# Recurrence of a hybrid block: a new order of TensorE's small and large groups of products

## Chip, cores, metric

One Trainium2 chip (trn2), one core. The metric is the device time of one execution in microseconds.

## The reference, cut to what matters

One layer for 1024 tokens of width 1024: RMSNorm, one input projection, an RWKV-7 group (8 heads of 64) beside a sliding-window attention group, an output projection, a SwiGLU feed-forward, a final norm. The change lies in the RWKV-7 recurrence:

```python
def step(S, inp):
    r_t, w_t, k_t, v_t, kk_t, a_t = inp
    sa = jnp.einsum('bhvk,bhk->bhv', S, -kk_t)
    S = (S * w_t[:, :, None, :]
         + sa[..., None] * (kk_t * a_t)[:, :, None, :]
         + v_t[..., None] * k_t[:, :, None, :])
    return S, jnp.einsum('bhvk,bhk->bhv', S, r_t)
...
o = (o - mean) * lax.rsqrt(var + GN_EPS)
```

## The kernel before, in words

The scan is done in 8 token tiles (t = 0 to 7) of 128 tokens. Within a tile the recurrence is a triangular system: NB and KB hold, for each head, the masked products of keys with queries (part 0) and with the removal keys (part 1); the inverse of the triangular part is built from 16x16 blocks on VectorE (`lanes`, the block inverse), and grown on TensorE to 32 (corners 1, updates 1: y1 and x1) and 64 (corners 2, updates 2: y2). U solves the tile, S is the state, O the output.

All engines run their own instruction list, written out by hand; semaphores order them. PSUM has eight banks, and a plan (`C`) gives each job of a tile a bank: O always has bank 5, R bank 0, t1 bank 1, U and t2 bank 2, y1 and y2 bank 4, x1 bank 6. `C.claim` lets TensorE wait until the reader of the job before in that bank has emptied it; `C.result` lets a reader wait for the products; `C.emptied` waits for the reader.

TensorE in tile t (`stage5_tensor`): products of the state with alpha into R (L1497); a filler, `busy`, a matmul with the identity that nobody reads (L1456); corners 1 (L1416), which wait for X; KB's products with V, part 1, into R (L1491); the claim of O; updates 1 (y1, then x1, L1416); the running sums of the decay gates for tile t+2 (`cumulative`, L1250, which reads sgt); part 0 of KB's products for heads 0 to 3 into O; corners 2; part 0 for heads 4 to 7; updates 2 (y2); the state with rho into O; `outputs(t-1)`, four transposes (L1468); U in two halves with the corrections of R between (L1542 to L1565); the new state (L1576); O's last products (L1582); the masks' raw products for later tiles (L1262).

VectorE in tile t (`stage5_vector`): Ts1 from corners 1 (L1658); `moments(t-1)`, which reads and empties O's bank (a sum, L1743, and the centred oc, L1746); `first_updates` of X and XT (L1664, L1665); `variance(t-1)` (L1754), which waits for ScalarE's squares of oc; `prepare(t+2)` (L1288 to L1294), which waits for ScalarE's exponentials of the running sums; `lanes(t+1)`; `gated`; the state's sum (L1776); the masks of KB for t+1 and of NB for t+2 (L1312).

ScalarE copies between: squares, R's low half, the exponentials, Ts2 from corners 2, XT from y2 (`last_updates`, L1606 and L1607), U and R.

SP's queue issues the transfers through DRAM: `gather` takes NB's diagonal blocks to the lanes (LA), `scatter` takes the inverse blocks (LM) to X and XT, and between them sgt (gates of tile t+2) and vtk (V of tile t+1) are loaded. GpSimd makes the reciprocal root of the variance, `on` and `mix`.

Of the kernel before, what the change touches and what calls it, by code (L numbers as in the profile page):

```python
# [17 lines left out]
NT = T // P  # L18
KD = D // P
HD = 64  # L20
H = 8
# [55 lines left out]
def hybrid_block(nc, x_t, par_in, w_in, w0, w_up, a_up, g_up, sinks, w_out, w_gate_up, w_down, norm_final_g,  # L77
# [13 lines left out]
    sg_dram = nc.dram_tensor("sg_scratch", (T, W), F32, kind="Internal").ap()  # L91
# [7 lines left out]
    with root:  # L99
# [1132 lines left out]
        def tok(t):  # L1232
            return slice(t * P, (t + 1) * P)
# [82 lines left out]
        def stage5_sync(sp):  # L1316
            def gather(t):

                for g in range(4):
                    C.emptied(sp, f"b{g}", t)  # L1320
                if t:
                    sp.wait_ge(s_lane, 16 * t)
                for q in range(2):
                    r = slice(q * HD, (q + 1) * HD)
                    sp.dma_start(bass.AP(d_n.tensor, q * (P + 1) * HD, [[P, HD], [8 * IMG, H], [1, HD]]),
                                 NB[t % 2][r, :, 1, r]).then_inc(s_img, 16)
                sp.wait_ge(s_img, 32 * t + 32)
                if t:
                    sp.wait_ge(s_inv16, t)
                sp.dma_start(LA[:, 0:BLK * BLK].rearrange("p (i j) -> p i j", i=BLK),  # L1330
                             bass.AP(d_n.tensor, 0, [[IMG, 64], [P, BLK], [1, BLK]])).then_inc(s_lane, 16)

            def scatter(t):
                sp.wait_ge(s_inv16, t + 1)
                if t:
                    sp.wait_ge(s_xt, 32 * t)
                sp.dma_start(bass.AP(d_i.tensor, 0, [[IMG2, 64], [P, 2 * BLK], [1, BLK]]),
                             LM.rearrange("p (r j) -> p r j", j=BLK)).then_inc(s_img2, 16)
                if t:
                    C.result(sp, "t2", t - 1)  # L1340
                else:
                    A.result(sp, "rn", NT - 1)
                sp.wait_ge(s_img2, 16 * t + 16)
                for m, o, done in ((X, P, s_xl), (XT, 0, s_xt)):
                    if t and m is XT:
                        C.result(sp, "U", t - 1)
                    for q in range(2):
                        sp.dma_start(m[q * HD:(q + 1) * HD, :, :],
                                     bass.AP(d_i.tensor, o + q * (2 * P + 1) * HD, [[2 * P, HD], [8 * IMG2, H], [1, HD]])
                                     ).then_inc(done, 16)  # L1350

            A.result(sp, f"sc{NP - 1}", NT - 1)
            sp.dma_start(sgt[:, :], sg_dram[tok(1), :]).then_inc(s_sgt, 16)
            sp.wait_ge(s_vd, 16 * NT)
            sp.dma_start(vtk_[0][:, :], v_dram[tok(0), :]).then_inc(s_vtk, 16)
            gather(0)
            scatter(0)
            for t in range(NT):
                if t + 2 < NT:
                    C.result(sp, "cum1", t + 1)  # L1360
                    sp.dma_start(sgt[:, :], sg_dram[tok(t + 2), :]).then_inc(s_sgt, 16)
                if t + 1 < NT:
                    gather(t + 1)
                    sp.wait_ge(s_vtk, 16 * t + 16)
                    if t:
                        C.result(sp, "S", t - 1)
                    sp.dma_start(vtk_[(t + 1) % 2][:, :], v_dram[tok(t + 1), :]).then_inc(s_vtk, 16)
                    scatter(t + 1)

        def cleared(pool, first, end):  # L1370
# [31 lines left out]
        def stage5_tensor(pe):  # L1402
# [6 lines left out]
            def blocks_of(b, count, lhs, rhs, groups):  # L1409

                n = len(groups) * H
                for h in range(H):
                    for g in groups:
                        lo, ro = lhs(g, h), rhs(g, h)
                        to = g[2]
                        mm = pe.matmul(b[32 * to:32 * to + 32, h * count:(h + 1) * count] if len(ro.shape) == 2 else  # L1416
                                       b[32 * to:32 * to + 32, h * count:(h + 1) * count].rearrange("p (a w) -> p a w", a=2),
                                       lo, ro, start=h == 0, stop=h == H - 1, skip_group_check=True)
                return mm

            def rows(g):
                return slice(32 * g, 32 * g + 32)
# [15 lines left out]
            def updates(n, t):  # L1438
                C.emptied(pe, f"t{n}", t)
                if n == 1:  # L1440
                    b = C.claim(pe, "y1", t)
                    C.done(blocks_of(b, 32, lambda g, h: Ts1[rows(g[0]), h, :],
                                     lambda g, h: XT[rows(g[0]), h, :].rearrange("p (a w) -> p a w", a=2)[:, :, 16:32], FOUR),
                           "y1", t)
                    b = C.claim(pe, "x1", t)
                    C.done(blocks_of(b, 16, lambda g, h: XT[rows(g[0]), h, 0:32],
                                     lambda g, h: Ts1[rows(g[0]), h, 0:16], [(0, 0, 0), (2, 0, 2)]), "x1", t)
                else:
                    C.emptied(pe, "y1", t)
                    b = C.claim(pe, "y2", t)  # L1450
                    C.done(blocks_of(b, 32, lambda g, h: Ts2[rows(g[0]), h, :],
                                     lambda g, h: XT[rows(g[0]), h, 32:64], [(1, 0, 0), (3, 0, 2)]), "y2", t)

            def busy(b, n):
                for _ in range(n):
                    pe.matmul(b[:, :], ident, cst[:, 0:HALF], start=True, stop=True)  # L1456
# [26 lines left out]
            for t in range(NT):  # L1483
# [5 lines left out]
                def products_of(b, part, *hs):  # L1489
                    for h in hs:  # L1490
                        mm = pe.matmul(b[:, h * HD:(h + 1) * HD], KB[:, h, part, :], vtk[:, h * HD:(h + 1) * HD],  # L1491
                                       start=part == 0 and h == 0, stop=False, skip_group_check=True)
                    return mm
# [12 lines left out]
                if not more:  # L1506
                    C.emptied(pe, "S", t - 1)
                    busy(bank[3], 3)
                if t:
                    if more:  # L1510
                        busy(C.claim(pe, "t1", t), 1)
                    corners(1, t)
                pe.wait_ge(s_vtk, 16 * t + 16)
                for g in range(4):
                    C.emptied(pe, f"k{g}", t)
                products_of(br, 1, *range(H)).then_inc(s_r, 1)
                bo = C.claim(pe, "O", t)
                if t == 0:
                    corners(1, t)
                    products_of(bo, 0, *range(4))  # L1520
                    busy(C.claim(pe, "S", t), 1)
                pe.wait_ge(s_xt, 32 * t + 32)
                updates(1, t)
                if t + 2 < NT:
                    cumulative(pe, t + 2)
                if t:
                    products_of(bo, 0, *range(4))
                corners(2, t)
                products_of(bo, 0, *range(4, H))
                updates(2, t)  # L1530
                if more:
                    of_state(bo, rho, False)
                else:
                    busy(bank[3], 1)
                if t:
                    outputs(t - 1)

# [115 lines left out]
        def stage5_vector(dve):  # L1653
# [75 lines left out]
                       "ot", t)  # L1729

            lanes(0)
            dve.wait_ge(s_z5, 6)
            masked(dve, "k", KB, 0, 0, 1)
            prepare(dve, 1)
            masked(dve, "k", KB, 0, 2, 3)
            A.emptied(dve, "pv", NT - 1)
            A.emptied(dve, "g", NT - 1)
            dve.wait_ge(s_gm, NT)
# [18 lines left out]
            for t in range(NT):  # L1757
                first_corners(t)
                if t:
                    moments(t - 1)  # L1760
                first_updates(t)
                if t:
                    variance(t - 1)
                if t + 2 < NT:
                    prepare(dve, t + 2)
                if t + 1 < NT:
                    lanes(t + 1)
                if t:
                    gated(t - 1)
                if t + 1 < NT:  # L1770
                    b = C.result(dve, "S", t)
                    if t:
                        dve.wait_ge(s_S, t)
                    for e in range(2):
                        r = slice(HD * e, HD * e + HD)
                        ins = dve.tensor_tensor(Sn[r, :, r], b[r, :].rearrange("p (a n) -> p a n", a=NP)[:, :, r],  # L1776
                                                S[r, :, r], ALU.add)
                    C.read(ins, "S", t)
                    masked(dve, "k", KB, t + 1, 0, 1, 2, 3)
                if t + 2 < NT:  # L1780
                    masked(dve, "b", NB[t % 2], t + 2, 0, 1, 2, 3)
# [918 lines left out]
```

## Time and profile before

| what | value |
|---|---|
| median of the three runs | 1307.79 us (1307.63 to 1317.0) |
| profiled execution | 1302.4 us, its span 1300.6 us |
| TensorE matmul busy | 1258.5 us, 97% of the span |
| VectorE, ScalarE, GpSimd busy | 830.2, 480.0, 271.8 us |
| granted TensorE clock, mean | 0.988 |
| recurrence (tiles 0 to 7) | about 354 to 552 us from the span's start |

The profile is one execution. "Idle before, <-releaser" in a timeline is how long the engine stood still before the row and who let it go on; "issue" means that nothing in the profile shows what it waited for. A float32 matmul is shown as two records. Rows of the timeline merge neighbouring records (xN).

### The profile page before, as it was taken

How to read it: one execution, taken by the hardware profiler on the slowest of the kernel's cores; microseconds unless marked ns; L12 is line 12 of the kernel's file. 1: busy time of each engine (PE TensorE's matmuls, PEld its weight loads, DVE VectorE, ACT ScalarE, POOL GpSimd, SP SyncE). 2: the span in 40 equal slices, each digit the busy share in tenths (PEclk: the TensorE clock that was granted, in tenths of full speed). 3: DMA queues.
4: the chain of work that ended last, by engine and by line, in shares of the span. 5: the costliest groups of instructions: out<-in, count | busy, mean ns of one | idle time of the engine just before them, and what ended most of it. 6: DMA issues, size and time to landing. Idle time of an engine off the chain costs nothing.

```text
span 1300.6 us, 20575 instructions
## 1 busy us (share of the span) xinstructions
PE 1258.5 (97%) x8219; PEld 1027.6 (79%) x8219; DVE 830.2 (64%) x1247; ACT 480.0 (37%) x863; POOL 271.8 (21%) x210
## 2 busy tenths in 40 slices
PE   7999999988899999999999999999999999999996
PEld 6888888655588888788878888888888888888885
DVE  6866622289868867554575666567677776547765
ACT  6100032398433323333453333333333334334335
POOL 0576600034302112100005233233223300000001
PEclk9999999999999989999999999999999999999998
DMA  5576632300232232332212321333554577766643
GB/s 218 188 249 216 224 107 100 116 1 8 50 65 49 62 69 54 126 155 98 86 54 87 98 77 70 98 100 111 194 174 142 170 274 273 235 212 211 213 142 138
DMA packets 117627, 172.80 MB, mean 133 GB/s; under 512 B 55328, under 2 KB 59424, under 8 KB 117280
## 3 DMA queue, kind: packets, MB, share of 16 engines
q1 hardware_dynamic: 117536, 171.54, 40.0%
q8 instruction: 63, 1.03, 0.3%
q14 instruction: 28, 0.23, 0.1%
HBM read 119.57 MB, written 51.39 MB: 131 GB/s over the span
## 4 chain that ended last, share of the span: by engine, by line
PE 83%; DVE 8%; DMA 4%; ACT 3%; issue 1%; SPq 0%; DVEq 0%; ACTq 0%
PE bank L2368 28%; PE bank L363 21%; PE bank L2472 14%; PE bank L1491 2%; PE bank L377 2%; PE bank L468 2%; PE bank L1416 2%; PE bank L1262 2%; DMA hid_scratch<-rt 1%; PE bank L1497 1%; PE bank L986 1%; DVE scores L1172 1%; PE bank L1456 1%; DMA inv_scratch<-LM 1%; DMA X<-inv_scratch 1%
## 5 line engine op out<-in xcount | busy, mean ns | idle before, releaser
L2368 PE MATMUL bank<-thi,ahi 128*128 128x512 f32 x320 | 124.5, 389 | 0.0
L2368 PE MATMUL bank<-tlo,ahi 128*128 128x512 f32 x320 | 124.5, 389 | 0.0
L2368 PE MATMUL bank<-thi,alo 128*128 128x512 f32 x320 | 124.5, 389 | 0.0
L2472 PE MATMUL bank<-ch,dwh 128*128 128x512 f32 x308 | 120.3, 391 | 0.4 <-DVE dwl L2046 0.4
L2472 PE MATMUL bank<-ch,dwl 128*128 128x512 f32 x308 | 119.9, 389 | 0.0
L2472 PE MATMUL bank<-cl,dwh 128*128 128x512 f32 x308 | 119.8, 389 | 0.0
L342 DVE TENSOR_TENSOR ring_wlo<-ring_raw,ring_whi 128x1024 fp32r<-128x1024 f32 x30 | 40.5, 1350 | 122.1 <-ACT ring_whi L336 122.1
L363 PE MATMUL bank<-hhi,ring_whi 128*128 128x512 f32 x288 | 114.4, 397 | 0.0
L363 PE MATMUL bank<-hhi,ring_wlo 128*128 128x512 f32 x288 | 112.2, 390 | 0.0
L363 PE MATMUL bank<-hlo,ring_whi 128*128 128x512 f32 x288 | 112.1, 389 | 0.0
L2368 PE MATMUL bank<-x1hi,ahi 128*128 128x512 f32 x240 | 93.4, 389 | 0.0
L2368 PE MATMUL bank<-x1lo,ahi 128*128 128x512 f32 x240 | 93.4, 389 | 0.0
L2368 PE MATMUL bank<-x1hi,alo 128*128 128x512 f32 x240 | 93.4, 389 | 0.0
L336 ACT ACTIVATE ring_whi<-ring_raw 128x1024 fp32r<-128x1024 f32 x30 | 31.6, 1056 | 152.5 <-PE bank L363 142.2
L2042 ACT ACTIVATE dwh<-dwr 128x1408 fp32r<-128x1408 f32 x28 | 38.7, 1381 | 114.1 <-PE bank L2472 107.8
L2368 PEld LDWEIGHTS bank<-tlo,ahi 128*128 128x128 f32 x320 | 60.1, 188 | 12.6
L2368 PEld LDWEIGHTS bank<-thi,ahi 128*128 128x128 f32 x320 | 60.1, 188 | 12.5
L2368 PEld LDWEIGHTS bank<-thi,alo 128*128 128x128 f32 x320 | 60.1, 188 | 12.4
L2472 PEld LDWEIGHTS bank<-ch,dwh 128*128 128x128 f32 x308 | 57.8, 188 | 12.8 <-DVE dwl L2046 0.8
L2472 PEld LDWEIGHTS bank<-ch,dwl 128*128 128x128 f32 x308 | 57.8, 188 | 12.2
L2472 PEld LDWEIGHTS bank<-cl,dwh 128*128 128x128 f32 x308 | 57.8, 188 | 11.7
L363 PEld LDWEIGHTS bank<-hhi,ring_whi 128*128 128x128 f32 x288 | 54.1, 188 | 11.9 <-issue 1.0
(341 smaller groups left out, 2805.4 us busy)
## 6 DMA issues: line engine op xcount, KB each, us to landing
hraw<-hid_scratch SPq DMA_DIRECT2D x12, 1024.0 KB, 6.3
hid_scratch<-hid SPq DMA_DIRECT2D x22, 512.0 KB, 6.3
hid_scratch<-rt SPq DMA_DIRECT2D x11, 1024.0 KB, 4.7
dwr<-down_sums SPq DMA_DIRECT2D x16, 704.0 KB, 4.1
ring_raw<-in_w_in SPq DMA_DIRECT2D x20, 512.0 KB, 4.1
raw_a<-in_w_gate_up SPq DMA_DIRECT2D x20, 512.0 KB, 4.0
raw_b<-in_w_gate_up SPq DMA_DIRECT2D x20, 512.0 KB, 5.2
dwr<-in_w_down SPq DMA_DIRECT2D x12, 704.0 KB, 4.2
```

The lines of the kernel that those rows point to most:

```text
L336: act.activation(self.ring.hi[:, s, 0:self.kt, :], self.ring.raw[:, s, 0:self.kt, :], ACT.Copy).then_inc(self.ring.hi_ready, 1)
L342: dve.tensor_tensor(self.ring.lo[:, s, 0:self.kt, :], self.ring.raw[:, s, 0:self.kt, :], self.ring.hi[:, s, 0:self.kt, :].bitcast(F32), AL ...
L363: mm = pe.matmul(o[:, :], wpart[:, s, k, :], apart[:, k, c], start=i == 0, stop=i == n - 1)
L377: mm = pe.matmul(bank[self.J.bank_of[f"{s}{half}"]][:, :], wpart[:, s, ks[n], :], apart[:, ks[n], c], start=n == 0 and i == 0, stop=n == l ...
L468: mm = pe.matmul(b[:, :], wpart[:, s, k, :], apart[:, k, c], start=k == 0 and i == 0, stop=k == KD - 1 and i == 2)
L986: mm = pe.matmul(bank[6][HD * e:HD * e + HD, p * P:(p + 1) * P], vt[:, t + j, (p // 2) * HD:(p // 2 + 1) * HD], pt[:, p % 2, j, e, :], sta ...
L1262: mm = pe.matmul(b[e][:, i * 2 * P:(i + 1) * 2 * P].rearrange("p (a n) -> p a n", a=2), src[r, 2 * g + i, tok(t)], rho_alpha(t, r, 2 * g + ...
L1416: mm = pe.matmul(b[32 * to:32 * to + 32, h * count:(h + 1) * count] if len(ro.shape) == 2 else b[32 * to:32 * to + 32, h * count:(h + 1) * ...
L1491: mm = pe.matmul(b[:, h * HD:(h + 1) * HD], KB[:, h, part, :], vtk[:, h * HD:(h + 1) * HD], start=part == 0 and h == 0, stop=False, skip_g ...
L2042: act.activation(dw_hi[m % 2][:, :, :], dw_raw[m % 2][:, :, :], ACT.Copy).then_inc(ring2.hi_ready, 1)
L2368: mm = pe.matmul(b[:, :], w[:, k, :], m[:, k, :], start=opens and k == 0 and i == 0, stop=not (j, n) in parts and k == 3 and i == 2, skip_ ...
L2472: mm = pe.matmul(b[:, :], w[m % 2][:, k, :], a[:, k, :], start=opens and k == 0 and i == 0, stop=name not in PART2 and k == KF - 1 and i = ...
```

## The change

TensorE: corners 1 move behind KB's part 1; the filler before them (tiles 1 to 6) goes; part 0 for heads 0 to 3 moves up behind corners 1 and the claim of O; x1's update moves behind the running sums; part 0 for heads 4 to 7 moves ahead of corners 2; updates 2 move behind the state's products with rho. VectorE: `prepare(1)` moves ahead of the first masks, `variance(t-1)` ahead of `first_updates(t)`. SP: sgt for tile t+3 is issued between vtk and the scatter of tile t+1, instead of that for t+2 ahead of the gather.

```diff
@@ -1353,18 +1353,22 @@
             sp.dma_start(sgt[:, :], sg_dram[tok(1), :]).then_inc(s_sgt, 16)
             sp.wait_ge(s_vd, 16 * NT)
             sp.dma_start(vtk_[0][:, :], v_dram[tok(0), :]).then_inc(s_vtk, 16)
+            def gates(t):
+                C.result(sp, "cum1", t - 1)
+                sp.dma_start(sgt[:, :], sg_dram[tok(t), :]).then_inc(s_sgt, 16)
+
             gather(0)
             scatter(0)
+            gates(2)
             for t in range(NT):
-                if t + 2 < NT:
-                    C.result(sp, "cum1", t + 1)
-                    sp.dma_start(sgt[:, :], sg_dram[tok(t + 2), :]).then_inc(s_sgt, 16)
                 if t + 1 < NT:
                     gather(t + 1)
                     sp.wait_ge(s_vtk, 16 * t + 16)
                     if t:
                         C.result(sp, "S", t - 1)
                     sp.dma_start(vtk_[(t + 1) % 2][:, :], v_dram[tok(t + 1), :]).then_inc(s_vtk, 16)
+                    if t + 3 < NT:
+                        gates(t + 3)
                     scatter(t + 1)
 
         def cleared(pool, first, end):
@@ -1442,14 +1446,16 @@
                     C.done(blocks_of(b, 32, lambda g, h: Ts1[rows(g[0]), h, :],
                                      lambda g, h: XT[rows(g[0]), h, :].rearrange("p (a w) -> p a w", a=2)[:, :, 16:32], FOUR),
                            "y1", t)
-                    b = C.claim(pe, "x1", t)
-                    C.done(blocks_of(b, 16, lambda g, h: XT[rows(g[0]), h, 0:32],
-                                     lambda g, h: Ts1[rows(g[0]), h, 0:16], [(0, 0, 0), (2, 0, 2)]), "x1", t)
                 else:
                     C.emptied(pe, "y1", t)
                     b = C.claim(pe, "y2", t)
                     C.done(blocks_of(b, 32, lambda g, h: Ts2[rows(g[0]), h, :],
                                      lambda g, h: XT[rows(g[0]), h, 32:64], [(1, 0, 0), (3, 0, 2)]), "y2", t)
+
+            def update_of_x(t):
+                b = C.claim(pe, "x1", t)
+                C.done(blocks_of(b, 16, lambda g, h: XT[rows(g[0]), h, 0:32],
+                                 lambda g, h: Ts1[rows(g[0]), h, 0:16], [(0, 0, 0), (2, 0, 2)]), "x1", t)
 
             def busy(b, n):
                 for _ in range(n):
@@ -1506,32 +1512,27 @@
                 if not more:
                     C.emptied(pe, "S", t - 1)
                     busy(bank[3], 3)
-                if t:
-                    if more:
-                        busy(C.claim(pe, "t1", t), 1)
-                    corners(1, t)
                 pe.wait_ge(s_vtk, 16 * t + 16)
                 for g in range(4):
                     C.emptied(pe, f"k{g}", t)
                 products_of(br, 1, *range(H)).then_inc(s_r, 1)
+                corners(1, t)
                 bo = C.claim(pe, "O", t)
+                products_of(bo, 0, *range(4))
                 if t == 0:
-                    corners(1, t)
-                    products_of(bo, 0, *range(4))
                     busy(C.claim(pe, "S", t), 1)
                 pe.wait_ge(s_xt, 32 * t + 32)
                 updates(1, t)
                 if t + 2 < NT:
                     cumulative(pe, t + 2)
-                if t:
-                    products_of(bo, 0, *range(4))
+                update_of_x(t)
+                products_of(bo, 0, *range(4, H))
                 corners(2, t)
-                products_of(bo, 0, *range(4, H))
-                updates(2, t)
                 if more:
                     of_state(bo, rho, False)
                 else:
                     busy(bank[3], 1)
+                updates(2, t)
                 if t:
                     outputs(t - 1)
 
@@ -1729,10 +1730,9 @@
                        "ot", t)
 
             lanes(0)
+            prepare(dve, 1)
             dve.wait_ge(s_z5, 6)
-            masked(dve, "k", KB, 0, 0, 1)
-            prepare(dve, 1)
-            masked(dve, "k", KB, 0, 2, 3)
+            masked(dve, "k", KB, 0, 0, 1, 2, 3)
             A.emptied(dve, "pv", NT - 1)
             A.emptied(dve, "g", NT - 1)
             dve.wait_ge(s_gm, NT)
@@ -1758,9 +1758,8 @@
                 first_corners(t)
                 if t:
                     moments(t - 1)
+                    variance(t - 1)
                 first_updates(t)
-                if t:
-                    variance(t - 1)
                 if t + 2 < NT:
                     prepare(dve, t + 2)
                 if t + 1 < NT:
```

## Rows read from the trace of the kernel before

**Rows 1.** The page: busy time, share of the span and instructions of each engine.

```profile
PE 1258.5 (97%) x8219; PEld 1027.6 (79%) x8219; DVE 830.2 (64%) x1247; ACT 480.0 (37%) x863; POOL 271.8 (21%) x210
```

**Rows 2.** Stretches, one per tile (3, 4, 5): length, busy (instructions), clock, DMA.

```profile
429.30:453.80 24.50, 23.73 (x409) 20.73 (x407) 19.41 (x42) 7.85 (x22) 4.65 (x4) 1.00 0.31 67
453.80:483.20 29.40, 28.30 (x409) 25.00 (x407) 19.50 (x42) 7.83 (x22) 4.49 (x4) 0.83 0.34 77
483.20:506.90 23.70, 23.60 (x408) 20.70 (x406) 19.40 (x42) 7.85 (x22) 4.65 (x4) 1.00 0.18 35
```

**Rows 3.** Timeline of PE, tile 3: start, length, line, operation, idle before.

```profile
430.27 1.02 PE L1456 MATMUL bank<-cst 128*128 128x512 f32 x2
431.97 0.72 PE L1416 MATMUL bank<-X,NB 32*32 32x16 f32 x64 [0.67 <-DMA X<-inv_scratch]
432.67 1.97 PE L1491 MATMUL bank<-vtk,KB 128*128 128x64 f32 x16
434.62 0.72 PE L1416 MATMUL bank<-XT,Ts 32*32 32x32 f32 x62
...
435.78 1.16 PE L1250 MATMUL bank<-cst,sgt 128*128 128x129 f32 x8
436.77 1.00 PE L1491 MATMUL bank<-vtk,KB 128*128 128x64 f32 x8
...
439.36 0.69 PE L1416 MATMUL bank<-XT,Ts 32*32 32x32 f32 x32
439.99 1.16 PE L1497 MATMUL bank<-S,arv 128*128 128x128 f32 x8
441.05 0.63 PE L1468 MATMUL bank<-cst,on 128*128 128x128 f32 x4
```

**Rows 4.** Timeline of DVE in tile 3.

```profile
432.89 0.35 DVE L1658 TENSOR_SCALAR Ts<-bank,cst 128x128 f32<-128x128 f32 x1 [1.34 <-PE bank L1416]
433.16 0.68 DVE L1743 TENSOR_REDUCE sm<-bank 128x8 f32<-128x512 f32 x1
433.88 0.69 DVE L1746 SCALAR_TENSOR_TENSOR oc<-sm,bank 128x512 f32<-128x512 f32 x1
...
438.11 0.69 DVE L1288 TENSOR_TENSOR ab<-ab,einv 128x512 f32<-128x512 f32 x1 [0.94 <-ACT einv L1279]
...
448.28 0.37 DVE L1718 COPY LM<-LV 64x256 f32<-64x256 f32 x1
```

**Rows 5.** Timeline of PE: waits for X, and gaps by issue.

```profile
382.76 0.72 PE L1416 MATMUL bank<-X,NB 32*32 32x16 f32 x64 [0.73 <-DMA X<-inv_scratch]
...
386.58 0.22 PE L1416 MATMUL bank<-XT,Ts 32*32 32x32 f32 x3 [0.48 <-issue]
...
407.52 0.72 PE L1416 MATMUL bank<-X,NB 32*32 32x16 f32 x64 [0.25 <-DMA X<-inv_scratch]
...
460.60 0.20 PE L1416 MATMUL bank<-Ts,XT 32*32 32x16 f32 x2 [0.94 <-issue]
```

**Rows 6.** Timeline of ACT in tile 3: second copy of y2.

```profile
440.49 0.37 ACT L1607 ACTIVATE XT<-bank 32x256 f32<-32x256 f32 x1
```

**Rows 7.** Timeline of SP's queue: X for tile 4.

```profile
451.97 1.27 SPq L1348 DMA_DIRECT2D X<-inv_scratch  x2
```

**Rows 8.** Timeline of all engines, at the start of the recurrence.

```profile
347.47 1.35 DVE L1312 COPY_PREDICATED KB<-cst,bank 128x512 f32<-128x512 uint32 x2 [1.21 <-PE bank L1262]
...
351.25 3.29 PE L1262 MATMUL bank<-arv,ab 64*128 64x256 f32 x16 [1.79 <-DVE arv L1292]
```

**Rows 9.** Stretches in which the granted clock was at half.

```profile
461.00:471.00 10.00, 10.00 (x101) 9.30 (x101) 8.27 (x23) 2.71 (x11) 3.22 (x3) 0.50 0.18 35
...
515.60:519.00 3.40, 3.40 (x44) 3.17 (x38) 3.12 (x12) 0.75 (x2) 1.71 (x2) 0.50 0.14 42
...
539.50:543.00 3.50, 3.50 (x36) 1.92 (x28) 0.00 (x0) 1.80 (x3) 1.63 (x2) 0.51 0.48 159
...
351.90:355.20 3.30, 3.30 (x15) 2.10 (x12) 2.47 (x5) 0.00 (x0) 0.00 (x0) 0.50 0.74 182
```

## The prediction

> **What bounds the kernel now.** I read the page first. TensorE (PE) is busy 1258.5 us of a span of 1300.6 [rows 1], so whatever moves the time must shorten or lengthen PE's own queue. Everything that is changed lies in the recurrence, between 346 and 552 us. The table of stretches, one per token tile, says how a tile is bounded [rows 2]: tile 3 lasts 24.5 us with PE busy 23.73, tile 5 lasts 23.7 with 23.60. VectorE (DVE) is busy 19.4 of them and ScalarE 7.9. Tile 4 has the same instructions (409) and lasts 29.4 us: its granted clock is 0.83. So a tile costs PE's work at the full clock, some short waits, and now and then a stretch at half clock.
>
> The timeline of PE in tile 3 shows the order [rows 3]: a filler of 1.02 us, 0.67 us of idleness until X has landed, the first corners (431.97 to 432.67), KB's products by V (1.97 us), then the y1 and x1 products, the running sums (1.16), half of O's products, the second corners, the other half, y2, the state's products, the transposes, and U. At the same time DVE does, in this order, Ts1 from the corners (432.89) and then the moments of the tile before, 433.16 to 434.57 [rows 4]. The moments are what frees the bank of O, and they stand behind Ts1 in DVE's queue. In the kernel before, PE spends exactly this time on KB's products: they end at 434.6.
>
> **The change, part by part.** All sums are against the profiled execution, 1302.4 us.
>
> *Fillers out.* One filler in each of tiles 1 to 6 goes: start to start 1.0 us [rows 3], so -6.0 us of PE's time.
>
> *Corners behind KB's products.* KB's masks are made before the tile begins, so KB's 1.95 us can run right behind the alpha products, while X still lands. X was waited for 0.73, 0.25 and 0.67 us in tiles 1, 2, 3 [rows 3, 5]; KB's products, 1.95 us in place of the 1.0 us filler, cover that: -1.65.
> But right behind the corners now stands the claim of O's bank, then half of O's products. The claim waits for the moments of tile t-1, and those wait in DVE's queue behind Ts1, which waits for these same corners. By the row of DVE the moments end at 434.57 where the corners ended at 432.67 [rows 3, 4], so PE stands still for 1.9 us and the handover (0.05: one row ends at 351.19 for a start at 351.25): 1.95 us. What is queued behind that claim is all of PE's tile: O, y1, the sums, everything. The work that hid the moments has been moved in front of the corners and nothing took its place. +1.95 in each of tiles 1 to 7 = +13.65. From both sides: it can't be under 1.0 unless the moments shrink (two passes of 0.68 and 0.69 that have to be made after Ts1), and is at most 2.1.
>
> *Y2 last but one.* y2 now comes behind the state's products; between y2 and U stand the transposes alone. ScalarE copies y2 into XT until 440.86, that is 1.5 us from the start of y2 at 439.36 [rows 3, 6]. Before, the state's products and the transposes (1.06 + 0.6) covered that. Now y2 itself (0.6) and the transposes (0.6) are 1.2 us: U waits +0.3 us in tiles 1 to 7, and 0.9 in tile 0, which has no transposes: +3.0. Bounds 1.5 and 4.
>
> *x1 behind the running sums, variance before the first updates.* The sums come 0.6 us sooner after y1, x1's update as much later; the first updates end about 5.9 us after the corners, where the exponentials that preparation waits for are ready too, against 5.4 before [rows 4]. Variance waits for ScalarE's squares, in a time in which DVE had nothing to do. Nothing of it is on PE's path: 0. The cover is the DVE's slack before X, next.
>
> *The loop through X.* Corners of t, Ts1, y1, sums, exponentials, preparation, the block inverse (ends 448.65), scatter, X at 451.97 issued and about 4 us later landed [rows 4, 7]: at present 23.9 to 24.5 us. With the 1 us wait and the shifts above it becomes about 24.8 us from corners to corners. PE's own tile becomes 23.85 - 1.0 + 1.95 + 0.3 = 25.1. So X is no longer late; the loop costs nothing, and would take over only if DVE's part grew by 0.4 us.
>
> *sgt a tile ahead.* Its issue (0.62) moves on SP's queue from before the gather to between vtk and the scatter. There it waits for the sums of tile t+2, which PE has made some 12 us before the scatter's own release; so the scatter isn't delayed. Before, the gather began right after B's masks, not after sgt. 0, bounds -0.3 and +0.3.
>
> *Preparation moved up, at the start.* DVE idles 1.21 us, makes two masks (347.47 to 348.8), then prepares tile 1; PE idles 1.79 us until that ends [rows 8]. With preparation (2.5 us) begun at 346.25 it ends at 348.8, and the two masks, which then gate PE through the banks, end at 350.15: -1.1 us. The clock was at half for 3.3 us right behind that idleness (351.9 to 355.2, [rows 9]); if the shorter idleness spares that, -1.5 more. I take -2.6, bounds 0 and -2.8.
>
> *The gaps without a releaser.* PE stood 0.48 and 0.94 us inside the run of y1 and x1 products (96 small matmuls in a row), with nothing that released it [rows 5]. With large groups between, I take both as gone: -1.4; bounds -1.4 and +1. The Trainium skill ("Runtime: NRT & Kernel Launch", instruction fetch mechanics) says that straight code is fetched ahead and that this is hidden; by that rule the gaps have another cause, and splitting the groups removes nothing: the sum would be 1.4 us more. The row, two gaps where matmuls are shortest and none in large groups, speaks rather for a supply that runs short.
>
> At full clock the sum is -6.0 - 1.65 + 13.65 + 3.0 - 2.6 - 1.4 = +5.0 us.
>
> *The clock.* This is the large and uncertain term. The granted clock went from full (2.4 GHz) to half (1.2) four times [rows 9]: after the 1.79 us of idleness; in tile 4, after KB's products, y1, x1 and the 0.94 us gap, and then for 10 us; in tiles 6 and 7 for 3.4 and 3.5 us after y1, x1, half of O, the second corners, half of O and with no idleness. What these have in common is small products, half-loaded groups of O or KB, and short idleness, close together; tiles 1 to 3, which had less of it, kept the full clock. The change puts into every tile KB's products, corners, 1.95 us of nothing, half of O and y1 in a row: 6 us with less work than what preceded each fall. So I expect a fall in most tiles, in spite of the spread small groups. Price of a fall: half of its length, 1.7 us (3.4 at half clock) to 5.0 us (10 us). The nearest row is tile 4's, since the new fall too comes ahead of the sums and the second half of O, not just before the state's products: 5.0. I take five such falls in the seven tiles, +25, in place of the three of before (5.0 + 1.7 + 1.75 = 8.45). Net +16.5; bounds -8.45 (no fall at all) and +26.5 (seven long ones).
>
> Sum: 1302.4 + 5.0 + 16.5 = 1324 us. The profiled run was 5.4 us below the median of the runs shown, 1307.79; against that median the forecast is +1.2%.
>
> **Rivals.**
> *The clock behaves as before.* The 1.95 us wait is there, but spreading the small groups offsets it: two or three falls of the old sizes. Then 1302.4 + 5.0 = 1307, no change. For it: tile 1 had 0.73 us of idleness and a 0.48 us gap around the corners and kept its clock [rows 5]. Against: the new hole is 2.7 times as long. It decides from about three long falls down.
> *No fall at all.* 1307.4 - 8.45 = 1299, -0.7%. This is what the order would give if small groups in a row were the only cause of the falls.
> *The hole isn't there.* This is the other side: PE doesn't wait for the moments, because DVE gets at them early enough or O's bank is free. Mechanism: only the claim of bank 5; price: 13.65 us less and then also no new falls: 1299 - 13.65 = 1285, and the loop through X, 24.2 us a tile, then binds and gives back some 6 us: about 1291, -1.3%. It turns on one thing, DVE's order of Ts1 and moments, and the rows speak against it.
> *Every tile falls long.* 1302.4 + 5.0 - 8.45 + 35 = 1334.
>
> **How the numbers follow.** Forecast (falls in most tiles, 1316 to 1340 with its bounds) 0.60; clock as before 0.25; no fall 0.10; no hole 0.05. The range has to reach into the second case: 1303 to 1340. A measurement of this kernel tells about 1% from no change, which is 1294.7 to 1320.9. Within the forecast's case about a tenth ends below 1320.9. Slower 0.55, within 1% 0.39, faster 0.06.
>
> **What the profile after would show.** PE idle about 1.9 us in front of O's products by V in tiles 1 to 7, released by DVE's oc; no wait for X; U waiting about 0.3 us for XT; PE's idleness at 350 us shorter by 1.1; stretches of tiles 1 to 5 of 25 us where the clock is 1.00 and 28 to 31 where it isn't; gaps by issue gone. I am wrong if the clock row shows 1.00 in most tiles, or if the claim of O's bank isn't waited for.

## The result, and the profile after

The changed kernel takes 1357.64 us (median of 4 runs, 1350.11 to 1366.22) against 1312.39 for the one before (median of 4 runs, 1307.63 to 1318.85), a ratio of 1.034 (95% interval 1.025 to 1.044). The ratios here and below are of fast executions: those more than 1.5% above the fastest of their kernel are left out. The profiled execution took 1351.6 us, 49.2 more than that of before (1302.4).

The stretches of the recurrence by tile, changed kernel, tiles 0 to 6 (length; busy us of PE, PEld, DVE, ACT, POOL with instructions; granted clock; DMA share; GB/s), answer to [rows 2]:

```profile
355.00:379.20 24.20, 23.20 (x403) 20.27 (x401) 14.01 (x35) 7.21 (x21) 0.00 (x0) 1.00 0.27 61
379.20:415.80 36.60, 34.75 (x407) 31.27 (x405) 18.68 (x42) 7.96 (x22) 4.17 (x4) 0.63 0.25 53
415.80:442.50 26.70, 24.48 (x407) 21.85 (x405) 18.62 (x42) 7.84 (x22) 4.17 (x4) 0.94 0.18 39
442.50:472.50 30.00, 28.08 (x412) 25.17 (x411) 19.32 (x43) 7.84 (x22) 4.15 (x4) 0.83 0.31 68
472.50:508.00 35.50, 33.65 (x401) 30.36 (x399) 17.79 (x41) 7.96 (x22) 4.15 (x4) 0.62 0.22 45
508.00:536.00 28.00, 25.78 (x418) 23.07 (x414) 19.90 (x45) 7.73 (x22) 4.15 (x4) 0.94 0.20 42
536.00:570.00 34.00, 31.54 (x375) 27.66 (x375) 15.02 (x34) 5.30 (x12) 4.15 (x4) 0.60 0.20 42
```

Read the clock column first, then the length: PE's work is about the same in tiles 1 to 5 (401 to 418 records), tile 0 at full clock takes 24.2 us, and no tile from 1 on stays at 1.00. VectorE is busy 17.8 to 19.9 us in each of tiles 1 to 5, whatever their length. The whole stage, changed kernel:

```profile
354.00:601.00 247.00, 231.69 (x3146) 202.68 (x3145) 134.90 (x288) 61.97 (x157) 29.99 (x28) 0.75 0.24 57
```

and before:

```profile
354.00:552.00 198.00, 192.73 (x3166) 164.96 (x3162) 139.31 (x289) 61.62 (x157) 32.30 (x28) 0.95 0.30 70
```

These two rows hold the result: 49 us more between about the same two points of the program, with PE idle 15 instead of 5 us, and the other 39 us of the growth in busy time of the same work (six fillers less) at a lower clock.

PE's timeline in tile 1, changed kernel (answers to [rows 3]; the last bracket is the idle time before the row and its releaser):

```profile
380.21 1.90 PE L1497 MATMUL bank<-vtk,KB 128*128 128x64 f32 x16
382.03 0.72 PE L1420 MATMUL bank<-X,NB 32*32 32x16 f32 x64
384.61 1.97 PE L1497 MATMUL bank<-vtk,KB 128*128 128x64 f32 x8 [1.85 <-DVE oc L1746]
386.51 1.08 PE L1420 MATMUL bank<-XT,Ts 32*32 32x32 f32 x64
387.52 2.09 PE L1250 MATMUL bank<-cst,sgt 128*128 128x129 f32 x8
389.54 1.04 PE L1420 MATMUL bank<-Ts,XT 32*32 32x16 f32 x32
390.50 1.75 PE L1497 MATMUL bank<-vtk,KB 128*128 128x64 f32 x7
```

and DVE's in the same place (answers to [rows 4]):

```profile
382.89 0.35 DVE L1659 TENSOR_SCALAR Ts<-bank,cst 128x128 f32<-128x128 f32 x1 [1.40 <-PE bank L1420]
383.16 0.68 DVE L1743 TENSOR_REDUCE sm<-bank 128x8 f32<-128x512 f32 x1
383.87 0.69 DVE L1746 SCALAR_TENSOR_TENSOR oc<-sm,bank 128x512 f32<-128x512 f32 x1
```

KB's products, the corners, then 1.85 us of nothing, until the moments have emptied O's bank at 384.56. Half of O's products takes 1.97 us for the 8 records that take 1.00 in [rows 3]: the clock has fallen inside the hole. The stretches around the fall and the rise:

```profile
383.00:384.00 1.00, 0.00 (x0) 0.00 (x0) 0.97 (x3) 0.00 (x0) 0.00 (x0) 1.00 0.69 148
384.00:385.00 1.00, 0.39 (x2) 0.39 (x3) 0.56 (x1) 0.35 (x1) 0.00 (x0) 0.73 0.48 100
385.00:411.00 26.00, 26.00 (x279) 23.32 (x278) 11.98 (x31) 5.99 (x18) 4.17 (x4) 0.50 0.24 49
411.00:412.00 1.00, 1.00 (x7) 1.00 (x7) 1.00 (x2) 1.00 (x4) 0.00 (x0) 0.61 0.00 0
```

For 26 us PE is busy without a break, and at half clock (1.2 GHz). A stretch whose clock reads 0.73 was at half clock for 0.54 of its microsecond; such parts are added up here. Taken over one-microsecond stretches from 346 to 609 us, the changed kernel is at half clock for 129.7 us: 27.3, 3.4, 10.2, 27.3, 3.4, 27.3 and 30.7 us, one fall in each of tiles 1 to 7. The kernel before has 23.9 us: five falls, four of them of 3.4 us. The prediction knew four; the fifth, at 553 us, comes behind the recurrence.

The start of the recurrence, changed kernel (answers to [rows 8]):

```profile
351.27 2.00 PE L1262 MATMUL bank<-arv,ab 64*128 64x256 f32 x16 [0.67 <-DVE KB L1312]
```

The wait for preparation is 0.67 in place of 1.79 us, and the products behind it take 2.00 in place of 3.29 us: no fall there. That the shorter wait spared the fall isn't shown. The kernel before without its fillers (below) waits the old 1.79 us and has no fall either:

```profile
351.18 2.00 PE L1262 MATMUL bank<-arv,ab 64*128 64x256 f32 x16 [1.79 <-DVE arv L1292]
```

### The profile page after: what moved, and what is told of

It reads as the page before. It is cut to its first block, busy times and chain, and to the rows that moved or that the text cites. A ratio compares the mean times of both kernels' runs of the same rounds, so it can differ in the third digit from the quotient of the medians.

```text
span 1349.8 us, 20544 instructions
## 1 busy us (share of the span) xinstructions
PE 1300.3 (96%) x8207; PEld 1068.0 (79%) x8207; DVE 826.0 (61%) x1247; ACT 480.5 (36%) x863; POOL 271.1 (20%) x210
## 3 DMA queue, kind: packets, MB, share of 16 engines
q8 instruction: 63, 1.03, 0.3%
## 4 chain that ended last, share of the span: by engine, by line
PE 92%; DVE 5%; ACT 2%; issue 1%; DMA 1%; DVEq 0%; SPq 0%; ACTq 0%
PE bank L2367 28%; PE bank L363 21%; PE bank L2471 16%; PE bank L1497 3%; PE bank L1262 3%; PE bank L1420 2%; PE bank L377 2%; PE bank L468 2%; PE bank L1503 2%; PE bank L1583 1%; PE bank L1250 1%; PE bank L986 1%; PE bank L1543 1%; PE bank L1566 1%; PE bank L1557 1%
## 5 line engine op out<-in xcount | busy, mean ns | idle before, releaser
L363 PEld LDWEIGHTS bank<-hlo,ring_whi 128*128 128x128 f32 x288 | 54.1, 188 | 12.0 <-issue 1.0
```

The source lines that it names most:

```text
L363: mm = pe.matmul(o[:, :], wpart[:, s, k, :], apart[:, k, c], start=i == 0, stop=i == n - 1)
```

## The experiments

Each ratio is to the kernel before, run beside it on the same chip. Three chips were used, on which the kernel before took 1310.4, 1305.7 and 1310.3 us, so ratios compare better than times. Half-clock times are those of one profiled execution each, between 346 and 609 us. **Theory A**: the hole in front of O's products is the cause of both the waiting and the falls. **Theory B**: the clock falls because the fillers are gone and small and half-loaded groups alternate, whatever the hole. **Theory C**: the waiting costs more than its length by its place.

**One part alone: corners behind KB's products, fillers kept** (on the kernel before).

```diff
-                if t:
-                    if more:
-                        busy(C.claim(pe, "t1", t), 1)
-                    corners(1, t)
+                if t and more:
+                    busy(C.claim(pe, "t1", t), 1)
...
+                corners(1, t)
                 bo = C.claim(pe, "O", t)
+                products_of(bo, 0, *range(4))
...
```

> The kernel before with one part of the change alone: corners 1 behind KB's products, and the first half of O's products right behind the claim, fillers kept, all else as before. Theory A: the whole loss appears, hole of 1.9 us in each of seven tiles (+12 after the waits for X that it hides) and long stretches at half clock: 1330 to 1350 us. Theory B (fillers taken out are what the clock misses): clock as before, about 1315 us.

Measured: 1360.26 us, ratio 1.040 (1.032 to 1.048). PE in tile 1:

```profile
384.63 1.89 PE L1491 MATMUL bank<-vtk,KB 128*128 128x64 f32 x16
386.46 0.73 PE L1416 MATMUL bank<-X,NB 32*32 32x16 f32 x64
388.97 1.97 PE L1491 MATMUL bank<-vtk,KB 128*128 128x64 f32 x8 [1.78 <-DVE oc L1742]
```

The same hole in all seven tiles, and the whole loss, with every filler in its place: 119.5 us at half clock, a fall in each of tiles 1 to 7 and one at the start. A's range (1330 to 1350 us) was too low by 10 us at its upper end. Missing fillers aren't the main cause: they were kept, and the clock fell as in the changed kernel.

**The other part alone: fillers out** (on the kernel before).

```diff
                 if t:
-                    if more:
-                        busy(C.claim(pe, "t1", t), 1)
                     corners(1, t)
```

> The kernel before without its fillers in tiles 1 to 6, nothing else. Theory A (what counts is idleness next to small groups): the 1.0 us of the filler turns mostly into waiting for X (the loop through X stays 24 us), so the full-clock time falls by 1 to 2 us at most and the half-clock stretches grow somewhat: 1300 to 1320 us. Theory B (the missing fillers are what the clock lacks): half-clock stretches of over 80 us as in the changed kernel, 1335 to 1355 us.

Measured: 1305.08 us, ratio 1.000 (0.996 to 1.004). What PE does where the filler was, tile 1:

```profile
378.64 1.16 PE L1497 MATMUL bank<-S,arv 128*128 128x128 f32 x8
381.17 0.71 PE L1416 MATMUL bank<-X,NB 32*32 32x16 f32 x64 [1.37 <-DMA X<-inv_scratch]
```

The filler turned into waiting for X, 0.9 to 1.4 us in five tiles. Half clock: 30.7 us against 23.9. This idleness in front of the corners cost next to nothing, as A had it (1300 to 1320 us).

**Everything but TensorE's order** (TensorE as before; preparation 1, variance and sgt as changed).

> The changed kernel with TensorE's order of before: of the change only preparation 1 ahead of the masks, variance ahead of the first updates and sgt a tile ahead are left. All theories: the loss is in TensorE's order, so this is the kernel before less 1.1 to 2.6 us at the start, 1303 to 1312 us. If sgt's or variance's move had a share in the loss, it would show here as over 1320 us.

Measured: 1306.0 us, ratio 1.000 (0.995 to 1.005). None of these three has a share in the loss. The start's gain isn't visible over the spread of the runs: this profile has one fall of 23.9 us in tiles 3 and 4, with TensorE's order of before and no hole. One of the ten runs took 4370.27 us, and one of the ten without fillers 2514.9; the cause of these two isn't known.

**The hole filled** (changed kernel, two fillers in front of the claim).

```diff
                 corners(1, t)
+                if t:
+                    busy(C.claim(pe, "S", t) if more else bank[3], 2)
                 bo = C.claim(pe, "O", t)
```

> The changed kernel with two filler matmuls (about 1.9 us at full clock) between the corners and the claim of O, in tiles 1 to 7: TensorE's queue is as long as with the hole, but it isn't idle. Theory A: the full-clock length stays (the wait turns into fillers), the half-clock stretches go: 1351.6 - 35 = 1310 to 1322 us. Theory C (the waiting itself, by its place in the chain, costs more than its length): stays above 1335 us.

Measured: 1303.21 us, ratio 0.995 (0.992 to 0.999); profiled execution 1301.3 us. From tile 4 to the end of the stage:

```profile
455.10:551.00 95.90, 93.06 (x1550) 77.02 (x1548) 64.46 (x130) 30.77 (x70) 17.52 (x16) 1.00 0.32 80
```

The clock doesn't fall between 346 and 609 us. PE's queue is as long as with the hole (tile 1 is 25.3 us from one tile's alpha products to the next's; forecast for the hole 25.1), and 50 us are gone (1351.6 to 1301.3). This separates the two prices: with the hole's time kept and PE busy in it, the loss of the falls, 50 us, is gone. C is out: as much time is spent at the same place, and the extra loss is gone. B isn't tested here, since fillers are back; the moments first, below, tests it. The measured time lies below A's range (1310 to 1322 us), which had the clock at 35 us.

**Half of the hole filled** (one filler in the same place).

> The changed kernel with one filler (about 1 us) between the corners and the claim of O in tiles 1 to 7: about 0.85 us of the 1.85 us hole is left idle, the full-clock length is the same as with the whole hole or with two fillers. Theory A with a price that follows the idle time: half-clock stretches in between, some 30 to 60 us, 1315 to 1335 us. If only a long hole makes the clock fall: as with two fillers, about 1303 us.

Measured: 1303.9 us, ratio 0.996 (0.992 to 0.999). PE in tile 1, and the stage from tile 1 on:

```profile
381.28 0.73 PE L1420 MATMUL bank<-X,NB 32*32 32x16 f32 x64
381.94 1.13 PE L1462 MATMUL bank<-cst 128*128 128x512 f32 x2
383.87 1.10 PE L1497 MATMUL bank<-vtk,KB 128*128 128x64 f32 x8 [0.81 <-DVE oc L1748]
```

```profile
378.40:551.00 172.60, 162.87 (x2760) 138.55 (x2758) 121.12 (x253) 54.03 (x136) 30.01 (x28) 1.00 0.30 72
```

0.7 to 0.8 us idle in each of seven tiles and no fall in them. The price doesn't follow the idle time; my middle case (1315 to 1335) was wrong, the other (about 1303) was right. The filler here both shortens the idleness and adds a large group, and the two aren't told apart by it.

**Corners ahead again** (changed kernel, corners 1 ahead of KB's products in tiles 1 to 7).

```diff
+                if t:
+                    corners(1, t)
                 pe.wait_ge(s_vtk, 16 * t + 16)
...
                 products_of(br, 1, *range(H)).then_inc(s_r, 1)
-                corners(1, t)
+                if t == 0:
+                    corners(1, t)
```

> The changed kernel with the corners ahead of KB's products again (tiles 1 to 7), everything else as changed, no filler. KB's products hide the moments again, but the corners come right behind alpha's products and wait for X: about 1 to 1.7 us idle per tile. Theory A (idleness around small groups makes the clock fall): some falls, fewer than in the changed kernel, 1305 to 1325 us. Theory B (order of groups without fillers): as bad in clock as the changed kernel, about 1335 us.

Measured: 1305.36 us, ratio 0.994 (0.989 to 0.998). PE in tile 3:

```profile
432.52 0.72 PE L1420 MATMUL bank<-X,NB 32*32 32x16 f32 x64 [1.62 <-DMA X<-inv_scratch]
433.22 3.03 PE L1497 MATMUL bank<-vtk,KB 128*128 128x64 f32 x24
```

No wait for the moments: O's first 8 records follow KB's 16 in one row. Three waits for X (1.62, 0.52, 0.62 us), 34.1 us at half clock. KB's products hide the moments again, and the loss is gone without a filler, as A had it (1305 to 1325 us); B had about 1335.

**The moments first** (changed kernel; the hole closed from VectorE's side).

```diff
-                first_corners(t)
                 if t:
                     moments(t - 1)
+                first_corners(t)
+                if t:
                     variance(t - 1)
```

> The changed kernel with VectorE's moments of the tile before ahead of Ts1, so that O's bank is free when TensorE claims it. Theory A (the hole in front of O's products is the cause of both losses, the 13 us of waiting and the long stretches at half clock): no wait for oc on TensorE, clock at half in at most three short stretches, 1351.6 - 13 - some 35 = 1295 to 1308 us. Theory B (the clock falls because the fillers are gone and small and half-loaded groups alternate through the tile, whatever the hole): only the wait goes, about 1338 us, half-clock stretches as in the changed kernel.

Measured: 1291.29 us, ratio 0.989 (0.985 to 0.993). Once more, beside the variants below:

> The kernel with the moments first once more, beside the two others that build on it. Expected 1291 to 1300 us, 1% under before.

Measured: 1291.99 us, ratio 0.990 (0.984 to 0.995). PE and DVE in tile 1 of that run:

```profile
379.80 1.90 PE L1497 MATMUL bank<-vtk,KB 128*128 128x64 f32 x16
381.62 0.75 PE L1420 MATMUL bank<-X,NB 32*32 32x16 f32 x64
382.43 1.10 PE L1497 MATMUL bank<-vtk,KB 128*128 128x64 f32 x8
383.46 0.75 PE L1420 MATMUL bank<-XT,Ts 32*32 32x32 f32 x64
384.15 1.15 PE L1250 MATMUL bank<-cst,sgt 128*128 128x129 f32 x8
385.23 0.68 PE L1420 MATMUL bank<-Ts,XT 32*32 32x16 f32 x32
385.84 0.32 PE L1497 MATMUL bank<-vtk,KB 128*128 128x64 f32 x1
```

```profile
380.97 0.68 DVE L1743 TENSOR_REDUCE sm<-bank 128x8 f32<-128x512 f32 x1
381.68 0.69 DVE L1746 SCALAR_TENSOR_TENSOR oc<-sm,bank 128x512 f32<-128x512 f32 x1
382.52 0.35 DVE L1659 TENSOR_SCALAR Ts<-bank,cst 128x128 f32<-128x128 f32 x1
```

The moments run while PE makes KB's products and end with the corners; Ts1 isn't late. O's products follow the corners directly, tiles 1 and 2 take 23.5 and 23.8 us, and this profile shows no half clock in the recurrence. TensorE's list is that of the changed kernel to the last instruction, without a filler; only the hole is gone. So B (about 1338 us) is out. The first median, 1291.29, lies 4 us below A's range (1295 to 1308).

The kernel isn't immune: another execution of it (1312.2 us) had 58.0 us at half clock, with falls of up to 27.3 us. The two executions give an estimate of the price: 1312.2 - 1289.7 = 22.5 us for 58.0 us, about 0.4 us for each us at half clock. The hole's falls have much the same price: 50.3 us for 129.7.

**The claim later** (changed kernel; O's claim and first half behind the running sums).

```diff
                 corners(1, t)
-                bo = C.claim(pe, "O", t)
-                products_of(bo, 0, *range(4))
...
                     cumulative(pe, t + 2)
+                bo = C.claim(pe, "O", t)
+                products_of(bo, 0, *range(4))
                 update_of_x(t)
```

> The changed kernel with the claim of O and the first half of O's products moved behind the running sums, VectorE's order as changed. It closes the hole from TensorE's side. Theory A: TensorE waits about 0.5 us for Ts1 in place of 1.85 for the moments; 1290 to 1310 us and few stretches at half clock. Theory B: about 1338 us.

Measured: 1313.89 us, ratio 1.009 (1.005 to 1.013), 54.6 us at half clock. PE in tile 4:

```profile
455.54 0.81 PE L1420 MATMUL bank<-X,NB 32*32 32x16 f32 x64
456.86 0.74 PE L1420 MATMUL bank<-XT,Ts 32*32 32x32 f32 x64 [0.51 <-issue]
457.53 1.16 PE L1250 MATMUL bank<-cst,sgt 128*128 128x129 f32 x8
```

Far below B's 1338, but above A's range (1290 to 1310). The wait for the moments is gone but for 0.5 us in the last tile; 0.5 us for Ts1 now stand between two small groups in each tile, and two long falls came late in the stage. So the hole is the main cause and not the only thing that makes the clock fall.

**Two more versions.** y2 ahead of the state's products (on the moments first), and the same with one filler behind the corners. The diff shows y2's part alone:

```diff
-                products_of(bo, 0, *range(4, H))
+                products_of(bo, 0, 4, 5)
                 corners(2, t)
+                products_of(bo, 0, 6, 7)
+                updates(2, t)
                 if more:
                     of_state(bo, rho, False)
...
-                updates(2, t)
```

> The kernel with the moments first, and y2 ahead of the state's products again (two heads of O on either side of the second corners). It takes away the waits before U (0.9 us in tile 0, 0.3 in the others, about 3 us). Expected 1291.3 - 3 = 1288 us, and without the stretch at half clock that followed the 0.9 us in tile 0, 1284 us. If the second corners or y2 now wait for their copies (0.4 us each), it gives this back: 1291.

> The kernel with the moments first and y2 ahead of the state's products once more, beside the one it builds on: 3 us less than that by the waits before U, up to 8 us less if the stretch at half clock behind tile 0's wait is gone too.

> The kernel with the moments first and y2 ahead of the state's products, with one filler behind the corners in tiles 1 to 7. Costs 7 us at full clock; by theory A it can win back only what that kernel still loses at half clock (17 us of half clock, 8.5 us lost, in its profile). Expected within 3 us of it, more even from run to run.

Measured: y2 ahead 1295.21 (ratio 0.994, 0.991 to 0.998) and again 1294.48 (0.995, 0.991 to 0.999); with a filler 1294.97 (0.990, 0.987 to 0.993). The waits before U are gone, but no time is won over the moments first (0.990 beside it): my 3 us don't show in the medians. The profiled execution of the second y2 ahead took 1289.3 us with 6.8 us at half clock, that of the moments first 1289.7 with none; at 0.4 the first would be some 2.7 us shorter without its falls. This is an estimate from two executions. The filler version is the steadiest, 11 of its 12 runs lie between 1294.0 and 1299.2; those of y2 ahead without it between 1289.3 and 1306.9. A gap without a releaser is still there, in tile 1 of the second y2 ahead, inside y1's group alone:

```profile
382.16 0.67 PE L1420 MATMUL bank<-XT,Ts 32*32 32x32 f32 x54
384.02 0.31 PE L1420 MATMUL bank<-XT,Ts 32*32 32x32 f32 x10 [1.19 <-issue]
```

The best version measured is the moments first: one line moved on VectorE turns a kernel 3.4% slower than before into one 1.0% faster (interval 0.5 to 1.6).

## Why the prediction was wrong, point by point

**The hole was right.** Forecast 1.95 us in each of tiles 1 to 7, released by oc; measured 1.78 to 1.85 us each. That it carries the loss is shown from both sides: by adding it to the kernel before, and by taking it out of the changed one in three ways, two of them without a filler.

**The full-clock sum was right.** Without falls I had 1299 us; the kernel with the hole filled, whose clock never fell, took 1301.3 in its profile. The hole's time was a little over-priced: without it (moments first, 1289.7) the time is 11.6 us shorter, not 13.65. X is no longer waited for. U waits 0.91 us in tile 0 and 0.32 in tiles 2 and 5, as forecast (0.9 and 0.3); in the other tiles, where the clock is at half ahead of U, no such wait shows. The start gave 1.1 us less waiting and no fall, but the second need not come of the first, as said above. The loop through X didn't take over.

**The clock was the step that failed, in size.** I took five falls of 5.0 us each, 25 us; there were seven, of up to 30.7 us of half clock, and together they cost 50 us (1351.6 - 1301.3). That a fall would come in most tiles, at the hole, was right. Its length wasn't: I priced it by the longest of before, 10 us, and took even the upper bound (seven such, 35 us) from it. Four of the seven stayed at half clock for over 27 us, the first of them with PE busy for 26 us without a break. With 50 in place of 25 the sum is 1349, and the profiled run is 1351.6.

Two errors stand in this term, and they pull against each other. Five falls of 10 us are 50 us of half clock, and 129.7 were measured. "Half of its length" was too dear: it would make 65 us of these 129.7, and 50 were measured, 0.39 of the length. Not every group takes twice as long at half clock. From start to start, tile 1 of the changed kernel against tile 1 of the moments first, O's first half takes 1.90 for 1.03 us and the running sums 2.02 for 1.08, but y1's small products 1.01 for 0.69 and x1's 0.96 for 0.61.

What I named as common to the falls of before was thin as well: tile 1 had more idleness around its small groups (0.73 and 0.48 us) than tiles 6 and 7, which had none ahead of their falls, and it kept its clock.

**The baseline.** The sum was set against one execution that was below the median of its kernel; the four runs of each kernel spread over 11 us (before) and 16 us (changed). Falls that come in one execution and not in another fit that, as the moments first showed. That adds to the miss of the median (1357.64) and was in no bound. It isn't the main part: from median to median the growth is 45 us, where the sum had 21.5.

**The gaps.** I took 1.4 us for gone. In the changed kernel's profile they are gone from y1 and x1; in other versions with the same spreading they came back (1.19 us inside y1's 64 records). So splitting the groups doesn't remove them. What causes them stays open; the rule of the Trainium skill ("Runtime: NRT & Kernel Launch", instruction fetch mechanics) that straight code is fetched ahead is neither borne out nor refuted here.

**The rivals.** "The hole isn't there" had been priced at 1291 us; the kernel with the moments first, in which it isn't, takes 1291 to 1292. That agreement is in part luck: 6 us of the 1291 were to come from the loop through X, at 24.2 us a tile, and this kernel's profile has no wait for X and tiles of 23.5 us. "Clock as before" and "no fall" are what the filled hole shows, not the changed kernel. "Every tile falls long" (1334) was the nearest and still too low, by the length that it gave a fall.

**Open.** Why a fall lasts 3.4 us in one tile and 27 in another of the same instructions wasn't settled. Nor is the point from which idleness costs a fall: 0.8 us behind the corners cost none with a filler beside it, 0.9 to 1.4 us ahead of the corners cost little, 1.8 us behind them cost one in every tile. Long falls aren't peculiar to the hole: 23.9 us came with TensorE's order of before, 23.9 with the corners ahead, 27.3 with the moments first and with the claim later. What the hole did in both kernels that have it is bring a fall in every one of seven tiles.

## What to carry to other kernels

When a group of work is moved on one engine, ask what it was hiding: name what the next claim waits for on the other engine, and where that stands in its queue. Here the reader of the bank came behind the very products that had been moved next to the claim, and moving that reader up, not another filler, is what paid. Price a fall of TensorE's clock with a wide upper end: the longest one in a profile with few falls is no bound for a kernel that has one in every tile. Other executions and near variants show how long they can get.

## What the hardware showed that I had not expected

TensorE stayed at half clock for 26 us while busy 26.00 of 26.00 us (the row above); in the profile before, the longest stretch was 10 us. With all other instructions in the same order, two fillers per tile in place of 1.85 us of idleness took the half-clock time from 129.7 us to 0, and one filler with 0.8 us of idleness to 3.4, a fall at 552 us, behind the recurrence. Half a clock isn't half a speed here: a microsecond at half clock cost about 0.4 us of time, both in the changed kernel and between two executions of the moments first.
